# First-layer probabilities: 32x32 turns on VectorE and a trip through memory in place of TensorE transposes

## The reference

```python
def _attention_layer(...):
    h = _rmsnorm(x, pre_g) * (1 + scale) + shift
    proj = h @ w_in
    ...
    outA = _dense_attention(qA, jnp.concatenate([kA, kA_c], axis=1), ...)
    outB = _window_attention(_rope(qB, cos, sin), _rope(kB, cos, sin), vB, kB_c, vB_c, sink)
    y = jnp.concatenate([outA, outB], axis=-1) * jax.nn.silu(z)
    x = x + gate * _rmsnorm(y @ w_out, post_g)
```

## Time and profile before

| | |
|---|---|
| median of three runs | 2537.72 us |
| profiled execution, first to last instruction (span) | 2534.0 us |
| around the span, by the median | 3.7 us |
| TensorE busy | 2497.7 us (99%) |
| VectorE busy | 1623.8 us (64%) |
| ScalarE busy | 973.6 us (38%) |
| DMA, mean | 154 GB/s |

### The profile page before, as it was taken

One profiled execution on the slowest core, in us unless ns is written; L12 is line 12 of the kernel. 1 busy time (PEld: TensorE's weight loads), 2 busy tenths in 40 slices (PEclk: granted clock), 3 DMA queues, 4 the chain that ended last, 5 costly groups with the idle time before them and its releaser, 6 DMA issues.

```text
span 2534.0 us, 30108 instructions
## 1 busy us (share of the span) xinstructions
PE 2497.7 (99%) x11975; PEld 2020.2 (80%) x11975; DVE 1623.8 (64%) x2444; ACT 973.6 (38%) x1549; POOL 110.7 (4%) x117
## 2 busy tenths in 40 slices
PE   7999999999999999999999999999999999999999
PEld 4789777777777887888888887888888787887887
DVE  4456776677776768776776768456365577656532
ACT  4232444444444333432434333445455432333421
POOL 0000000000000114000000113000000000000000
PEclk8999999999999999999999999999999999999999
DMA  9955433434433754666645754323222245532342
GB/s 350 336 193 185 127 110 121 125 125 133 132 101 136 258 180 157 208 200 211 200 162 175 249 175 158 111 76 91 80 87 84 75 151 169 175 112 89 123 154 83
DMA packets 293133, 390.58 MB, mean 154 GB/s; under 512 B 11698, under 2 KB 221234, under 8 KB 289154
## 3 DMA queue, kind: packets, MB, share of 16 engines
q1 hardware_dynamic: 287184, 355.84, 43.5%
q0 software_dynamic: 5808, 32.84, 3.5%
q10 hardware_dynamic: 2, 0.00, 0.0%
HBM read 371.85 MB, written 16.78 MB: 153 GB/s over the span
## 4 chain that ended last, share of the span: by engine, by line
PE 89%; DVE 5%; DMA 2%; ACT 2%; issue 1%; SPq 1%; POOL 0%; DVEq 0%; ACTq 0%; POOLq 0%
PE G L2151 74%; PE OB L2151 6%; PE S L2151 6%; PE TB L2154 2%; PE TB L2151 1%; DMA MRAW<-in_ev_mod_w 1%; DMA MORE<-in_ev_mod_w 1%; DVE WLO L1634 1%; DVE MACC L1640 1%; DVE TT L1634 1%; ACT PB L1445 1%; DVE SM L1862 0%; SPq L1129 0%; PE OB L2154 0%; DVE Y L1634 0%
## 5 line engine op out<-in xcount | busy, mean ns | idle before, releaser
L2151 PE MATMUL G<-HHI,WLO 128*128 128x512 f32 x2560 | 1001.0, 391 | 0.0
L2151 PE MATMUL G<-HHI,WHI 128*128 128x512 f32 x1964 | 801.8, 411 | 0.5 <-DVE CLO L1640 0.5
L2151 PE MATMUL G<-HLO,WHI 128*128 128x512 f32 x1928 | 753.2, 391 | 1.6 <-DVE HLO L1640 1.4
L2151 PEld LDWEIGHTS G<-HHI,WLO 128*128 128x128 f32 x2560 | 480.7, 188 | 104.3
L1272 ACT ACTIVATE WHI<-RAW 128x1024 fp32r<-128x1024 f32 x282 | 297.5, 1056 | 560.9 <-PE G L2151 501.6
L1634 DVE TENSOR_TENSOR WLO<-RAW,WHI 128x1024 fp32r<-128x1024 f32 x282 | 344.5, 1222 | 234.9 <-ACT WHI L1272 233.0
L2151 PEld LDWEIGHTS G<-HHI,WHI 128*128 128x128 f32 x1964 | 370.9, 189 | 80.3 <-issue 6.7
L2151 PEld LDWEIGHTS G<-HLO,WHI 128*128 128x128 f32 x1928 | 363.1, 188 | 79.7 <-issue 6.7
L1640 DVE SCALAR_TENSOR_TENSOR MACC<-MWIDE,SC,MACC 128x512 f32<-128x512 f32 x420 | 320.4, 763 | 39.2 <-DMA MWIDE<-in_w_ada 12.8
L2151 PE MATMUL G<-HHI,WHITA 128*128 128x512 f32 x536 | 215.0, 401 | 0.0
L2151 PE MATMUL G<-HLO,WHITA 128*128 128x512 f32 x536 | 209.2, 390 | 0.0
(11 more groups left out here) (347 smaller groups left out, 3060.7 us busy)
## 6 DMA issues: line engine op xcount, KB each, us to landing
RAW<-in_w_in SPq DMA_DIRECT2D x128, 512.0 KB, 3.7
MWIDE<-in_od_mod_w SPq DMA_DIRECT2D x96, 512.0 KB, 4.1
MWIDE<-in_w_ada SPq DMA_DIRECT2D x96, 512.0 KB, 4.6
RAW<-in_ev_w_in SPq DMA_DIRECT2D x80, 512.0 KB, 3.5
RAW<-in_od_w_in SPq DMA_DIRECT2D x64, 512.0 KB, 3.9
MWIDE<-in_ev_mod_w SPq DMA_DIRECT2D x32, 512.0 KB, 3.8
RAW<-in_ev_w_out SPq DMA_DIRECT2D x32, 512.0 KB, 3.3
RAW<-in_od_w_out SPq DMA_DIRECT2D x32, 512.0 KB, 3.3
```

Source lines behind the costliest of these rows:

```text
L2151: return e.o.matmul(o, l, r, start=start, stop=stop, skip_group_check=True)
```

## The change

What goes: the 336 transposes on TensorE with their waits, the copies from `TB` and `OB` to `PT` on ScalarE, and the second `PB`.

What comes: `PB` is one tile of a whole head, 128 partitions by 24 key blocks by 128 queries (12 KB a partition). ScalarE writes the exponentials into it in runs of 32. VectorE scales a row as before (now one stage later in the list, `row_end`) and then turns it in 32x32 blocks, in place (`STREAM_TRANSPOSE`). Within each quarter of the partitions the keys of a block are then on the partitions, but of all 768 keys each quarter still holds its own share of queries. So SyncE writes the whole tile to a scratch tensor in device memory (`p_spill`, 1.5 MB, one transfer, stage `turn`, three steps after the last `row_end` of the head), waits for it, and reads it back in four transfers of 32 partitions with runs of 128 numbers (512 bytes) into `PT` (stage `turn_in`, four steps later). `pv` follows nine steps after that. In `PT` the queries stand in another order; `gate` reads `OB` by that order, and `pv` of banded heads takes four pieces of 64 or 96 columns in place of one. The last head is moved from `PB` to `PT` directly, by eight transfers on SyncE's queue and eight on ScalarE's, and its `pv` comes six steps later.

Since there is one `PB`, the exponential of a head's first row waits for the write of the head before (`pw`), and rows 4 to 7 of a pair, its second head, stand five steps later than before (four in the last pair): at t = 17, 20, 23 and 26 in place of 12, 15, 18 and 21. For rows 0 and 1 of a banded head the exponential is two operations, since the keys used don't lie next to each other in `PB`; their scaling and turn go over all 24 blocks.

Everywhere in the kernel, the low part of a chunk becomes a stage of its own (`low`), put into the list one chunk after its high part. The fourth high buffer is now always the same one, with the waits on its neighbours gone.

```diff
-    PB = [scratch(f"PB{i}", [P, 768], F32, 24 * K1 + i * 3 * K1) for i in range(2)]
+    PB = scratch("PB", [P, 24, P], F32, 24 * K1)
...
+    PS = [nc.dram_tensor(f"p_spill{i}", [P, 24, P], F32) for i in range(2)]
...
         def split_ahead(i):
+            while at["low"] < at["split"]:
+                low_next()
             while at["split"] < min(i + NS, len(chunks)):
                 split_next()
...
             for n in range(8):
-                later(3 * n, "rows", n)
+                later(3 * n + (0 if n < 4 else 5 if p < 7 else 4), "rows", n)
...
                         put("score", h, qt)
                         put("softmax", h, qt, n)
-                        two = len(score_jobs(h, qt)[1]) > 4
-                        late = 1 if a[0] % 4 == 0 else 0
-                        later(t + 4 + late, "turn", h, qt, n, 0, not two)
-                        if two:
-                            later(t + 5 + late, "turn", h, qt, n, 1, True)
+                        later(t + 1, "row_end", h, qt, n)
                         if qt == 3:
-                            later(t + 7, "pv", h)
+                            later(t + 4, "turn", h)
+                            if h < 15:
+                                later(t + 8, "turn_in", h)
+                            later(t + (17 if h < 15 else 10), "pv", h)
...
+    def p_rows(qt, kt0, kt1):
+
+        return PB[:, 4 * kt0:4 * kt1, 32 * qt:32 * qt + 32]
+
+    def move(e, h, r):
+
+        for q in range(4):
+            src = PB[32 * q:32 * q + 32, :, :].rearrange("p (k r) n -> p k r n", r=4)
+            e.o.dma_start(PT[32 * r:32 * r + 32, :, P * q:P * q + P], src[:, :, r, :]).then_inc(*ptd.up(h, by=16))
...
+            elif stage == "turn":
+                h, = a
+                e.wait_ge(v_sm, (h, 3, "turned"))
+                if h < 15:
+                    if h > 1:
+                        e.wait_ge(ptd, h - 2)
+                    e.o.dma_start(PS[h % 2].ap(), PB[:, :, :]).then_inc(*pw.up(h, by=16))
+                else:
+                    e.wait_ge(p_pv, h - 1)
+                    for r in (0, 1):
+                        move(e, h, r)
+            elif stage == "turn_in":
+                h, = a
+                e.wait_ge(pw, h)
+                if h:
+                    e.wait_ge(p_pv, h - 1)
+                src = PS[h % 2].ap().rearrange("(a i) (k r) n -> r i k a n", a=4, r=4)
+                for r in range(4):
+                    e.o.dma_start(PT[32 * r:32 * r + 32, :, :].rearrange("i k (a n) -> i k a n", a=4),
+                                  src[r]).then_inc(*ptd.up(h, by=16))
...
-                if n >= 2:
-                    e.wait_ge(p_turn, n - 2)
+                if h:
+                    e.wait_ge(pw, h - 1)
...
-                ts(PB[n % 2][:, lo:768], PB[n % 2][:, lo:768], rs, None, MUL).then_inc(*v_sm.up((h, qt, "p")))
+                ts(rows, rows, rs, None, MUL).then_inc(*v_sm.up((h, qt, "p")))
+                e.wait_ge(v_sm, (h, qt, "p"))
+                e.o.transpose(rows, rows).then_inc(*v_sm.up((h, qt, "turned")))
...
             elif stage == "pv":
                 h, = a
                 col = slice(kv_of(h) * P, kv_of(h) * P + P)
                 e.wait_ge(a_ev, ("v", 1, 2))
-                e.wait_ge(*tb)
+                e.wait_ge(ptd, h)
                 e.wait_ge(*ob)
```

More of the change, by code:

```diff
@@ L110, in build @@
         WLO.append(place(f"WLO{i}", [P, 4, 256], F32R, at)[0])
-    WHI3 = [place(f"WHI{i}", [P, 4, 256], F32R)[0] for i in range(3)]
+    WHI = [place(f"WHI{i}", [P, 4, 256], F32R)[0] for i in range(3)]
     MRAW, MWIDE = [], []
@@ L185, in build @@
     KHI.append(scratch("KHI3", [P, 768], F32R, 0))
-    QLO = scratch("QLO", [P, 2, SEQ], F32R, 42 * K1)
+    QLO = scratch("QLO", [P, 2, SEQ], F32R, 48 * K1)
     LS2 = [LS, LSB]
@@ L304, in build @@
         first_chunk.append(first_chunk[-1] + len(u))
[L306 to L317, removed]
     nat = [("c", 0), ("c", 1)] + [("x", i) for i in range(4)]
@@ L364, in make_plan @@
         gates = [[], [], []]
-        at = {"load": 0, "split": 0, "use": 0, "done": 0, "unit": 0, "pair": 0, "heads": False, "hold": False, "extra": ()}
+        at = {"load": 0, "split": 0, "low": 0, "use": 0, "done": 0, "unit": 0, "pair": 0, "heads": False, "hold": False, "extra": ()}
         scored = []
@@ L387, in split_next, with low_next, low_until @@
             at["split"] += 1
+        def low_next():
+            put("low", at["low"])
+            at["low"] += 1
         def split_ahead(i):
+            while at["low"] < at["split"]:
+                low_next()
             while at["split"] < min(i + NS, len(chunks)):
                 split_next()
+        def low_until(i):
+            while at["low"] <= i:
+                low_next()
         def step(gens):
@@ L745, in pair_task @@
                 yield
+                if p == 7 and t > 28 and last_y < KT - 1:
+                    put("y_split", 1, last_y, h_unit)
+                    last_y += 1
             if p == 7:
-                for k in range(12, KT):
-                    put("y_split", 1, k, h_unit)
-                    yield
+                put("y_split", 1, KT - 1, h_unit)
+                yield
         def first_splits(layer):
@@ L1082, in q_root_of, with by_block @@
         return QROOT[:, h % 2 * 4 + qt:h % 2 * 4 + qt + 1]
-    def runs_of(part):
-        runs = []
-        for x, (j, c0) in enumerate(part):
-            if runs and runs[-1][1] + runs[-1][2] == j:
-                runs[-1][2] += 1
-            else:
-                runs.append([x, j, 1])
-        return runs
+    def p_rows(qt, kt0, kt1):
[4 more added lines that the diff above has]
+            e.o.dma_start(PT[32 * r:32 * r + 32, :, P * q:P * q + P], src[:, :, r, :]).then_inc(*ptd.up(h, by=16))
+    def by_block(t):
+        return t.rearrange("p (b j) -> p b j", j=32)
     def operand(kind, layer, k):
@@ L1451, in act_program @@
             elif stage == "turn":
-                h, qt, n, part, final = a
-                bank = OB if part else TB
-                e.wait_ge(p_turn, (h, qt, part))
-                if h:
+                h, = a
+                if h == 15:
+                    e.wait_ge(v_sm, (h, 3, "turned"))
                     e.wait_ge(p_pv, h - 1)
-                runs = runs_of(score_jobs(h, qt)[1][4 * part:4 * part + 4])
-                for x, j, m in runs:
-                    cp(PT[:, j:j + m, qt * P:(qt + 1) * P],
-                       bank[:, x * P:(x + m) * P].rearrange("p (j n) -> p j n", j=m)).then_inc(
-                        *a_turn.up((h, qt, part)))
+                    for r in (2, 3):
+                        move(e, h, r)
             elif stage == "silu_a":
```

114 lines of the change are left out of this document (60 added, 54 removed).

## The result

The changed kernel takes 2569.7 us (median of 4 runs, 2566.7 to 2571.6) where the kernel before takes 2537.7 (2534.9 to 2538.5) beside it. The ratio is 1.0124 with a 95% interval of 1.0112 to 1.0137: 32 us slower. The prediction was 2543 with a range of 2515 to 2572. The direction and the range hold; the size does not, +32 where the sum said +5.6.

A forecast was written before the change was run, and what follows sets the result against it. The prediction took TensorE, busy 99% of the span, as the bound. New waits of 42.6 us less 37.0 for transposes gave +5.6 on a span of 2534.0; with 3.7 carried to the median, 2543 us, range 2515 to 2572.

The forecast's parts named there:

- Existing and new waits: TensorE's waits, nearly all on scores in the heads: 48.2 us in all, 5.6 of them existing already, so +42.6 us.
- the layout: Step-by-step timing of VectorE against TensorE in a pair: waits of 8.3 us per banded pair, 4.5 per dense pair.
- What a wait costs beyond what it shows: TensorE's time around a wait on a score, beyond the wait itself; the prediction had no term for it.
- The transposes: Heads: 336 transposes leave TensorE at 0.11 us each, all on the path, 37.0 us gained.
- The low parts: Chunks throughout the kernel: making the low part one chunk later costs 0, between -5 and +3 us.
- The clock: TensorE's granted clock behind waits; the prediction had no term for it.
- The trip through memory: Write 8 us and reads 10 us between a head's turns and its `pv`: hidden, except 3 us at the last head.
- The rival of the late trip: Reads land after 18 us, so TensorE stands 2.6 us at each `pv`: 2573 us, chance 0.15.
- the slow turn: A VectorE turn takes 1.8 us in place of 0.96, so each wait in a pair grows: 2568 us, chance 0.12.
- The forecast's own range: Whole kernel, the sum without the rivals: 2535 to 2552 us, chance 0.40.

The follow-up runs named there:

- combo3: Changed kernel, second head's query rotation behind row 2, low parts late only in heads and last layer, first head's rows a step later, row ends behind next maximum: 2505.0 us.
- turns_twice: Kernel before, with each of TensorE's 336 transposes of the probabilities issued twice: 2569.0 us.
- low_at_once: Changed kernel, with a chunk's low part queued right behind its high part again, as before the change: 2573.8 us.
- before_low_late: Kernel before, with only the low part of a chunk put a chunk later, as the change puts it: 2545.8 us.
- filler: Changed kernel, with useless matmuls put in front of the scores on which TensorE waits, heads 2 to 13: 2567.3 us.
- rope_later: Changed kernel, with the rotation of the second head's query moved from in front of row 0 to behind row 2: 2561.4 us.
- before_late_mixed: Kernel before, with low parts a chunk later in the heads and the last layer, at once between them: 2533.8 us.

## Why the prediction was right in direction and wrong in size

- **Existing and new waits (+42.6).** Right in the sum, 49.2 us against 48.2, and mostly in their places; that it is so near is in part luck. In a banded pair 2.25, 1.33, 1.84 and 2.14 us against 2.1, 2.6, 2.2 and 1.4; in a dense one 0.95, 1.80 and 0.65 against 1.1, 2.6 and 0.8, with 0.88 at row 6 that the layout had not. Pairs 1 to 6 wait 4.1 us less than forecast; pair 0 waits 4.6 in place of 0.8 (the layout left out the 1.8 that it has before already), and 2.3 are waits on `MACC` that nobody had listed. That VectorE's order and not its load is what counts was right as well: combo3 does the same work in another order and waits for 12.3 us (though the turns still cost 10.3 us there).
- **What a wait costs beyond what it shows (0).** Not in the sum. From the last product ahead of a row to the first behind it TensorE takes 1.26 us in a dense pair and 0.94 or 1.11 in a banded one when it needn't wait, and 1.51, 1.18 and 1.37 beside the wait when it must (rows in which the clock doesn't fall). So each wait costs about 0.25 us more than the view gives it. The changed kernel has 31 waits on scores in the heads where there were nine: 5.5 us.
- **The transposes (-37.0).** Right, as TensorE's own time, which is what a sum needs that counts the waits apart. In turns_twice the span grew by 32.7 us while 2.9 us of waits went, five of them, with 0.25 each: 36.9. What they are worth in the whole kernel before, 31.5, is another number, since the waits move with them.
- **The low parts (0, between -5 and +3).** This step failed. The reason was "after 800 us TensorE hardly waits, so there is nothing to win", which looks only at the gain; "11 us of cover for 1.2 us of work" holds between two chunks but not at the passages to the next layers, where VectorE has other work queued behind which the low part falls. The two passages cost 12.9 us by low_at_once and 13.2 by before_low_late, and the end gives 2 back: +11, outside the bounds. What the later place gains in the heads was in the layout already.
- **The clock (0).** This step failed as well: it is not in the sum at all, and no reason is given. Waits of about 2 us each, which the forecast had foreseen, bring falls of the granted clock: seven in the heads, 1.6 us of TensorE's time each, 11.2 in all. What would come back without them is less, since waits grow in their place: 4.6 us in pairs 1 to 6 by filler.
- **The trip through memory (0, and 3 at the last head).** Right for the changed kernel: 7.4 us for the write and 7.2 for the reads, against 8 and 10, and no wait on `PT`. But the write is less hidden than the term had it. It looked at the second head's write; the first head's is the tight one, with one wait of ScalarE here and four in rope_later (2.5 to 3.9 us). At the last head the 2.6 us are waits on `HLO`, its output's low part, which the term named as its smaller part. The rival of the late trip is out, as is the slow turn.

Sum, in TensorE's time: 5.6 + 1.0 (waits) + 5.5 (what they cost beyond) + 11.2 (clock) + 11 (low parts) + 1.4 (ahead of the heads) = 35.7, where the spans differ by 33.8. Why it is 1.9 too high stays open.

The time lies inside the range, but not by the forecast's reasons. The forecast's own range ended at 2552. From there to 2572 the range was held open by the slow turn and the late trip, and neither happened. That part is luck.

The Trainium skill, "VectorE: DVE Perf Modes", section "Rules for kernel authors", gives a 128x128 transpose to TensorE. This kernel does the same work for six such blocks by one VectorE instruction of 0.978 us, which turns 32x32 blocks, and a trip through memory. By the changed kernel the rule holds; by combo3, 32 us faster than the kernel with TensorE's transposes, it does not, and the measurement decides: where TensorE is the bound and VectorE is not, it is the order that settles it.

That combo3's order would also gain without the turned layout was not tried beyond before_late_mixed (2.9 us). What it could win there can be estimated from the kernel before: 5.6 us of waits in the heads, 0.25 more for each of the nine, and 2.0 at the end, 10 us in all. So by this estimate at least 21 of combo3's 32 us are the change's idea itself.

## What to carry to other kernels

When work goes from the engine that bounds a kernel to one that has room, ask at each place what stands in the queue of the receiving engine ahead of the instruction that the bounding engine waits for, and put only that ahead; here all of the work that was moved could stand behind it. Two edits in one change get a term each, and one that is costed at nothing has to be walked past every passage between phases, not only through the steady state. A change that has lost may be only an order away from a gain: in the order that came with it this one lost 32 us, and in combo3's, 65 us faster, it gained 32.

## What the hardware showed that I had not expected

- Behind some waits of 1.8 to 4.5 us TensorE's matmuls of 128x512 start every 0.43 us in place of 0.23, as from 623.1 to 626.5. Behind others nothing happens: after the 2.25 us that end at 678.33 the products start every 0.23 us at once. Useless matmuls in the waits bring the granted clock from 0.83 back to 1.00.
- A fall that takes 1.6 us of TensorE's time cost the kernel 0.7 us in each of two dense pairs, and two of them 3.1 in a banded one.
- One VectorE turn of 128x768 numbers takes 0.978 us, one of 512 takes 0.712, beside 0.621 and 0.486 for a scaling of the same numbers.
- With 203 in place of 118 GB/s of traffic in the heads a chunk of 512 KB lands after 6.6 us in place of 3.5, and TensorE waits for none of them there.
- A wait of TensorE on a score costs 0.25 us more than its idle time in the profile.
